# A state-space layer with a mixture of experts: state matrices kept as 64x64 blocks instead of zero-padded 128x128 ones, u in three groups of 128, weights loaded during the scan

## The chip, the core and the metric

The kernel runs on one core of one Trainium2 chip. The time is the device time of one execution in microseconds, and the number given for a kernel is the median of its runs. The engines are TensorE (PE: matmuls; PEld is its weight load), VectorE (DVE), ScalarE (ACT), GpSimd (POOL) and SyncE (SP, which here only issues transfers). All data is fp32, and each fp32 matmul shows as two matmul instructions and two weight loads in the trace.

## The reference

384 tokens of 1024 channels (128 context tokens, 256 latent ones) pass one layer:

```python
mod = silu(cond) @ w_ada + b_ada                   # 1024 x 6144; sh1, sc1, g1, sh2, sc2, g2
h = rms_norm(x, norm_mix) * (1 + sc1) + sh1
u = h @ w_in
x_re, x_im = einsum("blgh,gph->blgp", u_g, bb)     # 64 groups of 16 channels, 64 complex states each
h_t = a * h_(t-1) + x_t                            # forward and backward, complex, diagonal
y = u * d_skip + sum over directions of Re(C h)
m = val * sigmoid(gate),  val, gate = split(gelu(y) @ w_glu)
x = x + g1 * m
x = x + g2 * moe(rms_norm(x) * (1 + sc2) + sh2)    # 16 experts, top 2 of one group, 1024 -> 1024 -> 1024
```

The outputs are the tokens after a final norm and the final states of the context scan. The discretised a and B are computed on the chip from lam, log_dt and b.

## The kernel before

Each engine has its program written out by hand; semaphores join them, and within an engine the order is that of the text. The scan is done over chunks of L = 4 tokens: CC = 32 context chunks and CL = 64 latent ones, C = 96, with one empty column between them CX = 97. 64 groups are held as GP = 32 pairs: the two groups of a pair (index i) lie in partitions 0-63 and 64-127.

Order of the work, by its lines:

1. SyncE loads seven pieces of w_ada (1 MB each), x, the eighth piece, waits for piece seven to land (L287), and loads w_in. ScalarE's own queue loads b, c (each c in two transfers of 256-byte pieces) and ssm_d in eight transfers of single elements (L545 to L557), and only then ScalarE goes on to the squares of the first norm (L564). TensorE multiplies each w_ada piece with silu(cond) (L745), VectorE adds the bias, TensorE spreads the rows to all partitions (L751), VectorE modulates x.
2. TensorE transposes b and x (L782, L794), and makes u = h w_in (L819): for each of the L = 4 positions in a chunk and each half of w_in, 8 matmuls whose weights are the 96 tokens at that position (`hT[:, k, i:T:L]`). Between them it transposes four batches of tables (transpose_W, L809). VectorE meanwhile computes w_pow (w_part) and V (v_part), and last b_keep (L1240). ScalarE copies the transposed W blocks into `pt` (L591), two copies of 64 partitions to a bank.
3. `pt` holds one 128x128 block for each pair, direction and real/imaginary part: the 64x64 blocks of the two groups on its diagonal and zeros elsewhere. GpSimd writes the zeros (zero_blocks, L411 to L421). u is transposed to uT (L837), evicted by ScalarE and VectorE. The P matmuls (L853) then make the chunk inputs, 128x128 weights times 97 columns, and are evicted into S by ScalarE (L624) and VectorE (L1252) in turn.
4. VectorE scans S chunk by chunk (L1265 to L1286). Beside it TensorE makes the kernels K inside a chunk (L870), ScalarE copies them to `kpad` in ring slot 7 (L631), GpSimd adds `dskip`, a diagonal of ssm_d, to them (L432), and SyncE moves them by 32 small transfers into `tmat` (load_T). SyncE loads w_ada pieces 8 to 23 into ring slots 8 to 11, four at a time (L301 to L309), and load_T stands in its queue between pieces 15 and 16.
5. V is copied into zero-padded blocks too, `v_pad`, in ring slots 4 to 11 (L643, eight copies by ScalarE; zeros by GpSimd, L436 and L438); its second half waits for the last w_ada piece.
6. y_inside(k) (L879) multiplies uT by tmat in 64x64 blocks, y_state(k) (L886) adds v_pad times S, read as `S[:, d, d:d + CX, r, g]` with 128 elements from one column to the next. ScalarE applies GELU, TensorE brings the channels into order (L896), the GLU matmuls follow (L954), for which w_glu is loaded into ring slots 4 to 11, each as y_state(k) ends (L320).
7. Norm, routing and 16 experts, whose weights stream through the ring.

## Time and profile before

| | |
|---|---|
| median of 3 runs | 998.11 us (996.9 to 998.47) |
| span of the profiled execution | 997.0 us (the page gives no other time of it) |
| PE busy | 800.8 us, 80% |
| DVE busy | 329.0 us, 33% |
| ACT busy | 195.6 us, 20% |
| POOL busy | 98.2 us, 10% |
| packets under 512 B | 19384 of 78154 |

The span runs from the first to the last instruction. The busy share is an average over all stages: the stages above fill about the first 350 us, the GLU and the routing reach to about 480 us, and the experts take the rest. In the first part each engine has long idle stretches, so the trace is read there in order of time: what starts late, and which event came just before it. In a timeline row the bracket gives the idle time before the work and what ended it.

### The profile page before, as it was taken

What the parts mean: (1) busy time and instruction counts of PE and PEld (TensorE: products, weight loads), DVE (VectorE), ACT (ScalarE), POOL (GpSimd) and SP (SyncE); (2) the same over time, 40 slices, a digit from 0 to 9 for tenths busy, and PEclk for the clock granted to TensorE, in tenths of its full rate; (3) what the DMA queues carried; (4) which work ended last, traced back from release to release, by engine and by line L of the source; (5) the groups of instructions that cost most, each with busy time, mean ns of one, the idle gap of its engine ahead of it and who ended that gap; (6) DMA issues with size and microseconds to landing.
All of it is one profiled execution on the core that took longest, in us unless ns stands there. A gap on an engine that the chain in (4) does not pass through costs nothing.

```text
span 997.0 us, 19297 instructions
## 1 busy us (share of the span) xinstructions
PE 800.8 (80%) x7936; PEld 464.8 (47%) x7937; DVE 329.0 (33%) x894; ACT 195.6 (20%) x372; POOL 98.2 (10%) x109
## 2 busy tenths in 40 slices
PE   4158999970169999965999999999999999999750
PEld 0035668930039944534545455454553555545320
DVE  6149983699910002224021120211111121121116
ACT  0033316300230212210021120211111121121113
POOL 1020002067020010002000000000000000000000
PEclk8579999975579999986999999999999999999995
DMA  8910000440554570047999999999999999999924
GB/s 306 342 14 1 2 0 2 170 171 8 159 214 169 199 273 0 1 165 300 343 397 410 410 410 410 408 410 410 410 410 410 335 413 410 410 411 410 410 74 189
DMA packets 78154, 259.14 MB, mean 260 GB/s; under 512 B 19384, under 2 KB 19816, under 8 KB 73880
## 3 DMA queue, kind: packets, MB, share of 16 engines
q1 hardware_dynamic: 70840, 253.04, 65.0%
q10 hardware_dynamic: 5632, 2.18, 1.3%
q0 software_dynamic: 1632, 3.20, 0.9%
q8 instruction: 38, 0.62, 0.3%
q14 instruction: 12, 0.10, 0.0%
HBM read 252.49 MB, written 6.29 MB: 260 GB/s over the span
## 4 chain that ended last, share of the span: by engine, by line
issue 47%; DVE 3%; POOL 2%; DMA 2%; POOLq 1%; ACT 0%; SPq 0%; DVEq 0%
POOL y_scratch L495 1%; POOLq L513 1%; DMA slots<-slot_list 1%; DMA ring<-y_scratch 0%; DVE ring L1457 0%; DVE sreg L1446 0%; DVE sreg L1447 0%; POOL slot_list L469 0%; DVE sreg L1448 0%; POOL pool_tick L483 0%; DMA slot_list<-sreg,sloti 0%; DMA y_scratch<-vreg,sidx 0%; POOL sidx L488 0%; ACT sreg L723 0%; POOLq L512 0%
## 5 line engine op out<-in xcount | busy, mean ns | idle before, releaser
L995 PE MATMUL ps<-ring,vreg 128*32 128x512 f32 x2240 | 246.6, 599 | 14.1 <-issue 13.8
L995 PEld LDWEIGHTS ps<-ring,vreg 128*32 128x32 f32 x2240 | 74.6, 111 | 179.0 <-issue 179.0
L1017 PE MATMUL ps<-ring,vreg 128*32 128x256 f32 x2240 | 124.2, 380 | 17.0 <-ACT vreg L702 17.0
L1017 PEld LDWEIGHTS ps<-ring,vreg 128*32 128x32 f32 x2240 | 81.3, 110 | 56.0 <-issue 16.3
L745 PE MATMUL ps<-ring,silu_c 128*32 128x512 f32 x192 | 39.6, 925 | 72.8 <-DMA ring<-in_w_ada 72.8
L981 PEld LDWEIGHTS ps<-vreg,sreg 128*128 128x128 f32 x768 | 89.3, 196 | 14.2 <-issue 12.6
L981 PE MATMUL ps<-vreg,sreg 128*128 128x96 f32 x768 | 91.9, 281 | 1.5 <-DVE vreg L1378 1.5
L1408 DVE TENSOR_TENSOR vreg<-vreg,ps 128x256 f32<-128x256 f32 x48 | 17.4, 417 | 224.3 <-ACT vreg L697 224.3
L1418 DVE COPY vreg<-ps 32x256 f32<-32x256 f32 x96 | 40.7, 424 | 132.2 <-PE ps L1017 129.7
L954 PE MATMUL ps<-ring 128*128 128x512 f32 x192 | 83.1, 593 | 0.7 <-ACT ring L652 0.7
L709 ACT ACTIVATE vreg<-ps 32x256 f32<-32x256 f32 x96 | 35.9, 374 | 131.5 <-PE ps L1017 129.5
L819 PE MATMUL ps<-ring,sreg 128*96 128x512 f32 x128 | 58.0, 612 | 1.8 <-ACT sreg L609 1.0
L954 PEld LDWEIGHTS ps<-ring 128*128 128x128 f32 x192 | 36.2, 190 | 45.4 <-issue 44.5
L697 ACT ACTIVATE vreg<-ps 128x256 f32<-128x256 f32 x48 | 15.0, 384 | 210.7 <-PE ps L995 210.7
L745 PEld LDWEIGHTS ps<-ring,silu_c 128*32 128x32 f32 x192 | 4.8, 130 | 104.8 <-DMA ring<-in_w_ada 101.3
L483 POOL TENSOR_TENSOR pool_tick<-ident 1x1 f32<-1x1 f32 x32 | 5.9, 185 | 442.0 <-DVE vreg L1418 357.8
L886 PE MATMUL ps<-sreg,ring 128*128 128x97 f32 x256 | 44.7, 351 | 3.4 <-ACT ring L643 3.4
L1283 DVE TENSOR_TENSOR sreg<-sreg,scan_t 128x128 f32<-128x128 f32 x190 | 46.3, 285 | 1.1
L886 PEld LDWEIGHTS ps<-sreg,ring 128*128 128x128 f32 x256 | 43.8, 219 | 3.8 <-issue 3.6
L1299 DVE TENSOR_TENSOR vreg<-vreg,ps 128x512 f32<-128x512 f32 x6 | 4.1, 689 | 125.1 <-ACT vreg L677 125.1
L819 PEld LDWEIGHTS ps<-ring,sreg 128*96 128x96 f32 x128 | 31.9, 253 | 25.3 <-issue 22.9
L432 POOL TENSOR_TENSOR ring<-ring,dskip 128x256 f32<-128x256 f32 x1 | 36.3, 36312 | 46.3 <-issue 46.3
(257 smaller groups left out, 682.2 us busy)
## 6 DMA issues: line engine op xcount, KB each, us to landing
ring<-in_moe_w_gate SPq DMA_DIRECT2D x128, 512.0 KB, 11.8
ring<-in_moe_w_up SPq DMA_DIRECT2D x128, 512.0 KB, 13.2
ring<-in_moe_w_down SPq DMA_DIRECT2D x128, 512.0 KB
ring<-in_w_ada SPq DMA_DIRECT2D x24, 1024.0 KB, 8.8
ring<-in_ssm_w_glu SPq DMA_DIRECT2D x8, 1024.0 KB, 4.8
ring<-in_ssm_w_in SPq DMA_DIRECT2D x8, 512.0 KB, 12.5
ring<-y_scratch SPq DMA_DIRECT2D x6, 512.0 KB, 6.2
tmat<-ada_rows SPq DMA_DIRECT2D x4, 512.0 KB, 7.1
```

The costliest lines, as they stand in the source:

```text
L432: pool.tensor_tensor(kpad[:, :, :, 48:64], kpad[:, :, :, 48:64], dskip[:, :, :, :], ALU.add).then_inc(pool_k, 1)
L709: act.activation(yrow[32 * t:32 * t + 32, 256 * j:256 * j + 256], src, ACT.Copy).then_inc(y_ev, 1)
L745: last = pe.matmul(ps[ADA_BANK[b]][32 * j:32 * j + 32, :], silu_c[:, k, :], src[:, j * 512:(j + 1) * 512], start=(k == 0), stop=(k == KT - 1))
L819: last = pe.matmul(ps[4 + m % 2][0:C, :], hT[:, k, i:T:L], win[:, k, half * 512:(half + 1) * 512], start=(k == 0), stop=(k == KT - 1))
L886: last = pe.matmul(ps[k][:, q * CX:(q + 1) * CX], v_pad[:, 4 * k + q, d, r, :], S[:, d, d:d + CX, r, 4 * k + q], start=False, stop=(d == 1 ...
L954: last = pe.matmul(ps[2 * (m % 2) + part][:, :], yT[:, k, t * P:(t + 1) * P], ring[:, 4 + k, col:col + 512], start=(k == 0), stop=(k == KT ...
L981: last = pe.matmul(bank[:, col * CAP:(col + 1) * CAP], h2[:, t, k * P:(k + 1) * P], onehot[:, t, :], start=(t == 0), stop=(t == NT - 1))
L995: last = pe.matmul(ps[t][32 * j:32 * j + 32, :], xgT[:, k, 32 * t:32 * t + 32], w[:, :, 256 * j:256 * j + 256], start=(k == 0), stop=(k == ...
L1017: last = pe.matmul(ps[3 + t // 2][32 * dj:32 * dj + 32, 256 * (t % 2):256 * (t % 2) + 256], aT[:, t, c2, 32 * j:32 * j + 32], ring[:, KT + ...
L1283: step(tt(to, to, tb, ALU.add), False)
L1408: tt(act_a[:, t, :], sg[:, t, :], ps[t][:, 256:512], ALU.mult).then_inc(prod_done, 1)
L1418: cp(yrow[32 * t:32 * t + 32, 256 * j:256 * j + 256], src).then_inc(y_ev, 1)
```

## The change

- The state matrices lose their padding. `pt` now holds the 64x64 blocks alone, in ring slots 8 to 11; V is used where it lies. P and y_state take two matmuls of 64 rows and 64 columns for each former one. W's eviction is one copy of 128 partitions, into four banks in turn. The zeroing on GpSimd, the copies L643 and their waits go.
- c is loaded as it lies, one transfer each, and the C transposes become pairs of 64-column matmuls. ssm_d is loaded as 8 rows of 128 early on, and transposed by TensorE (`drow`, `dtab`).
- The skip term: 16 matmuls `i16` by `dskip` add it in PSUM after K; the addition on GpSimd goes.
- The 32 transfers to tmat move from SyncE's queue to ScalarE's, and kpad to ring slot 0.
- w_ada pieces 8 to 23 go to ring slots 4 to 7, and the first of them wait for u only. Half of w_glu is loaded after P, the other half as the last w_ada pieces are used. w_in no longer waits for piece seven.
- u: the tokens of positions 0 to 2 of all chunks form three groups of 96, and the 96 tokens of position 3 are split in three and appended, 32 to each, so that three groups of 128 columns are used. ScalarE's evictions of hT and u become two each.

```diff
-        pads = ring[:, 4:12, :].rearrange("p a b -> p (a b)").rearrange("p (n j) -> p n j", j=P)
-        pt = [pads[:, (1 - d) * 2 * GP:(2 - d) * 2 * GP, :].rearrange("p (g r) j -> p g r j", r=2) for d in range(2)]
-        v_pad = pads.rearrange("p (g d r) j -> p g d r j", d=2, r=2)
+        pt = ring[:, 8:12, :].rearrange("p a b -> p (a b)").rearrange("p (d g r s) -> p d g r s", d=2, g=GP, r=2)
...
-            sp.wait_ge(ld_ada[6], 16)
             for k in range(KT):
                 sp.dma_start(win[:, k, :], w_in[0, k * P:(k + 1) * P, :]).then_inc(ld_win, 16)
...
-            sp.wait_ge(pe_p, 16)
+            def load_glu(k):
+                sp.dma_start(ring[:, 4 + k, :], w_glu[0, k * P:(k + 1) * P, :]).then_inc(ld_glu, 16)
+
+            sp.wait_ge(pe_u, 6)
             for n in range(KT, 3 * KT):
                 b, k = divmod(n, KT)
-                if n == KT + 8:
-                    load_T()
+                if n == KT + 4:
+                    sp.wait_ge(pe_p, 32)
+                    for kk in range(4, KT):
+                        load_glu(kk)
                 if n >= KT + 4:
                     sp.wait_ge(pe_ada, n - 3)
-                sp.dma_start(ring[:, 8 + n % 4, :],
+                sp.dma_start(ring[:, 4 + n % 4, :],
                              w_ada[0, k * P:(k + 1) * P, b * UNIT:(b + 1) * UNIT]).then_inc(ld_late[n % 4], 16)
+            for k in range(4):
+                sp.wait_ge(pe_ada, 2 * KT + k + 5)
+                load_glu(k)
...
-            pool.tensor_tensor(kpad[:, :, :, 48:64], kpad[:, :, :, 48:64], dskip[:, :, :, :], ALU.add
-                               ).then_inc(pool_k, 1)
...
+            act.dma_start(drow[:, 0:P], ssm_d[0].rearrange("(m p) -> m p", p=P)).then_inc(ld_drow, 16)
...
-                for i in range(2):
-                    act.dma_start(cnat[r * DG:(r + 1) * DG, :].rearrange("p (h i s) -> p i h s", h=GS, i=2)[:, i],
-                                  cc.rearrange("a d (g i) h s -> i (a d g) h s", i=2)[i]).then_inc(ld_bc, 16)
-            for q in range(4):
-
-                for i in range(2):
-                    act.dma_start(dtab[32 * q:32 * q + 16, i, :], ssm_d[0].rearrange(
-                        "(m q i h) -> q i h m", m=8, q=4, i=2)[q, i], allow_slow_non_contiguous=True
-                        ).then_inc(ld_dtab, 16)
-
+                act.dma_start(cnat[r * DG:(r + 1) * DG, :], cc.rearrange("a d (g i) h s -> (a d g) (i h s)", i=2)
+                              ).then_inc(ld_bc, 16)
...
-                act.activation(hT[:, k0:k0 + 4, t * P:(t + 1) * P],
-                               ps[m % 2][:, :].rearrange("p (k n) -> p k n", k=4), ACT.Copy).then_inc(act_hT, 1)
+                src = ps[m % 2][:, :].rearrange("p (k c j) -> p k j c", k=4, j=L)
+                to = hT[:, k0:k0 + 4, :].rearrange("p k (a c) -> p k a c", a=3)
+                act.activation(to[:, :, :, 32 * t:32 * t + 32], src[:, :, 0:3, :], ACT.Copy)
+                act.activation(to[:, :, t, 96:P], src[:, :, 3, :], ACT.Copy).then_inc(act_hT, 1)
...
-                    for i in range(2):
-                        a = slice(64 * i, 64 * i + 64)
-                        act.activation(pt[d][a, g0:g0 + 8, r, a],
-                                       ps[2 * (w % 2) + i][a, :].rearrange("p (g s) -> p g s", s=NS), ACT.Copy
-                                       ).then_inc(act_pt, 1)
-            for m in range(8):
+                    act.activation(pt[:, d, g0:g0 + 8, r, :],
+                                   ps[w % 4][:, :].rearrange("p (g s) -> p g s", s=NS), ACT.Copy).then_inc(act_pt, 1)
+            for m in range(6):
...
+            act.wait_ge(act_k, 4)
+            for i in range(2):
+                for j in range(L):
+                    for q in range(4):
+                        dst = tmat[64 * i + 16 * j:64 * i + 16 * j + 16, q:GP:4, :]
+                        act.dma_start(dst, kpad[32 * q:32 * q + 16, i, :, (3 - j) * GS:(7 - j) * GS]
+                                      ).then_inc(ld_tmat, 16)
...
+            for i in range(2):
+                pe.transpose(ps[5][:, 8 * i:8 * i + 8], drow[:, GS * i:GS * i + P], ident[0:8, 0:8])
...
-                    last = pe.matmul(ps[4 + m % 2][0:C, :], hT[:, k, i:T:L], win[:, k, half * 512:(half + 1) * 512],
+                    last = pe.matmul(ps[4 + m % 2][:, :], hT[:, k, i * P:(i + 1) * P], win[:, k, half * 512:(half + 1) * 512],
...
-                        last = pe.matmul(ps[m % 8][:, o:o + CX], pt[d][:, g0 + gi, r, :], uT[:, g0 + gi, :],
-                                         start=True, stop=True)
+                        for i in range(2):
+                            a = slice(64 * i, 64 * i + 64)
+                            last = pe.matmul(ps[m % 8][a, o:o + CX], pt[a, d, g0 + gi, r, :], uT[a, g0 + gi, :],
+                                             start=True, stop=True)
...
+                    for q in range(4):
+                        a = slice(32 * q, 32 * q + 32)
+                        last = pe.matmul(bank[32 * q:32 * q + 16, 0:448].rearrange("p (m w) -> p m w", w=112)[:, :, 48:64],
+                                         i16[a, :], dskip[a, i, 4 * mq:4 * mq + 4, :], start=False, stop=True,
+                                         skip_group_check=True)
...
-                            last = pe.matmul(ps[k][:, q * CX:(q + 1) * CX], v_pad[:, 4 * k + q, d, r, :],
-                                             S[:, d, d:d + CX, r, 4 * k + q], start=False,
-                                             stop=(d == 1 and r == 1), skip_group_check=True)
+                            for i in range(2):
+                                a = slice(64 * i, 64 * i + 64)
+                                v = V[a, d * GP + 4 * k + q, r, 1 - d:5 - d, :].rearrange("p k h -> p (k h)")
+                                last = pe.matmul(ps[k][a, q * CX:(q + 1) * CX], v, S[a, d, d:d + CX, r, 4 * k + q],
+                                                 start=False, stop=(d == 1 and r == 1), skip_group_check=True)
```

## Rows read from the trace of the kernel before

**Rows 1.** The page's 40 slices of 24.9 us: GB/s moved by the transfers.
```profile
GB/s 306 342 14 1 2 0 2 170 171 8 159 214 169 199 273 0 1 165 300 343 397 410 410 410 410 408 410 410 410 410 410 335 413 410 410 411 410 410 74 189
```

**Rows 2.** Timeline, 33 to 64 us: start, duration, engine, line, operation, tiles, count [idle before].
```profile
35.63 1.93 PE L745 MATMUL ps<-ring,silu_c 128*32 128x512 f32 x8 [5.34 <-DMA ring<-in_w_ada]
...
57.55 0.17 DVE L1149 TENSOR_SCALAR stat<-stat 128x3 f32<-128x3 f32 x1 [27.62 <-ACT vreg L564]
...
59.13 9.20 PE L751 MATMUL ps<-ada,ring 128*128 128x512 f32 x16 [21.57 <-DVE ada L1155]
```

**Rows 3.** Timeline of ScalarE, 14 to 60 us: its DMA issues (ACTq).
```profile
17.23 2.96 ACTq L550 DMA_DIRECT2D vreg<-in_ssm_c_re  x2
20.22 14.93 ACTq L547 DMA_DIRECT2D vreg<-in_ssm_b_im  x1
...
44.78 9.11 ACTq L555 DMA_DIRECT2D dtab<-in_ssm_d  x8
```

**Rows 4.** Windows of 5 us: busy us by engine, granted clock, DMA share, GB/s.
```profile
10.00:15.00 5.00, 3.33 (x16) 0.40 (x16) 4.30 (x21) 0.40 (x2) 0.00 (x0) 1.00 1.02 427
...
20.00:25.00 5.00, 2.04 (x16) 0.20 (x8) 4.79 (x41) 0.00 (x0) 0.00 (x0) 0.50 1.06 261
...
35.00:40.00 5.00, 1.93 (x8) 0.20 (x8) 0.00 (x0) 0.00 (x0) 0.00 (x0) 0.50 1.06 374
```

**Rows 5.** Timeline, 112 to 190 us, and the first GLU matmuls.
```profile
112.89 34.66 PE L819 MATMUL ps<-ring,sreg 128*96 128x512 f32 x80
...
144.11 1.23 DVE L1240 COPY tmat<-sreg 128x2048 f32<-128x2048 f32 x1
...
161.13 0.41 DVE L1248 COPY ring<-ps 128x256 f32<-128x256 f32 x1
...
161.65 28.80 PE L853 MATMUL ps<-ring 128*128 128x97 f32 x256 [0.76 <-ACT ring L619]
...
350.90 55.17 PE L954 MATMUL ps<-ring 128*128 128x512 f32 x128 [0.68 <-ACT ring L652]
```

**Rows 6.** Timeline, 190 to 343 us, by engine: VectorE, GpSimd, SyncE, ScalarE, TensorE.
```profile
191.74 0.29 DVE L1275 TENSOR_TENSOR scan_t<-a4r,sreg 128x128 f32<-128x128 f32 x1
...
276.09 0.61 DVE L1283 TENSOR_TENSOR sreg<-sreg,scan_t 128x128 f32<-128x128 f32 x2
...
207.84 36.31 POOL L432 TENSOR_TENSOR ring<-ring,dskip 128x256 f32<-128x256 f32 x1 [46.27 <-issue]
...
244.18 20.70 SPq L297 DMA_DIRECT2D tmat<-ring  x32
...
289.22 7.44 ACT L643 ACTIVATE ring<-vreg 64x2048 f32<-64x2048 f32 x4 [15.11 <-PE ps L745]
...
270.24 1.93 PE L745 MATMUL ps<-ring,silu_c 128*32 128x512 f32 x8 [46.53 <-DMA ring<-in_w_ada]
...
287.62 1.53 PE L745 MATMUL ps<-ring,silu_c 128*32 128x512 f32 x8 [0.53 <-DMA ring<-in_w_ada]
289.08 4.25 PE L879 MATMUL ps<-ring,tmat 64*64 64x97 f32 x96
296.76 33.49 PE L886 MATMUL ps<-sreg,ring 128*128 128x97 f32 x192 [3.43 <-ACT ring L643]
...
337.33 5.58 PE L886 MATMUL ps<-sreg,ring 128*128 128x97 f32 x32
```

**Rows 7.** The x loads (line 284): issues, and microseconds from issue to landing.
```profile
L284 SPq DMA_DIRECT2D vreg<-in_x_sample x2: 445/454/463, 7.9 to 8.4; - x2
...
DMA to landing us min/median/max: 22.4/23.4/24.4
```

**Rows 8.** Windows around the start of y_state: as rows 4.
```profile
293.30:296.70 3.40, 0.03 (x2) 0.00 (x0) 0.00 (x0) 3.38 (x3) 3.08 (x1) 0.81 0.00 0
296.76:299.00 2.24, 2.24 (x11) 2.24 (x11) 0.00 (x0) 1.20 (x1) 0.00 (x0) 0.50 0.00 0
```

**Rows 9.** The page's part 6: issues, KB each, microseconds to landing.
```profile
ring<-in_w_ada SPq DMA_DIRECT2D x24, 1024.0 KB, 8.8
```

100 lines of the change are left out of this document (34 added, 66 removed).

## The prediction, made before the change was timed

> **What bounds the kernel now.** I read the page's slices first. From about 475 us the GB/s row stands near 410 to the end of the experts: that half streams expert weights, and the change touches nothing in it [rows 1]. Before it lies a chain of stages with holes in PE and in the transfers. So I followed the order of time through the first 350 us, engine by engine, and asked at each hole which wait ends last. There are three.
>
> Hole one, 37.6 to 59.1 us. PE has finished the eighth w_ada piece at 35.63 + 1.93 = 37.6, but its next work, the 16 spreading matmuls (L751), starts at 59.13, behind a VectorE chain that waited until 57.55 for ScalarE's squares (L564) [rows 2]. ScalarE was only issuing DMAs: c_re 2.96 us, b_im 14.93, then c_im, and ssm_d 9.11, to 53.9 [rows 3]. These c and ssm_d transfers are cut in pieces of 256 and 4 bytes. While they run the transfers give 261 GB/s at a full share (20 to 25 us) against 427 before [rows 4].
>
> Hole two is not idle: VectorE works from 65 us through the state-space tables to 145.34 (b_keep, L1240), and PE's u matmuls end at 112.89 + 34.66 = 147.55, side by side [rows 5].
>
> Hole three. The scan on VectorE runs from 191.74 to about 276.7; but y_state (L886) starts at 296.76, twenty microseconds later [rows 6]. It waits for ScalarE's copies into the padded blocks (L643, 289.22 + 7.44), which wait for PE's last w_ada piece (287.62 + 1.53), whose loads stood behind the 32 tmat transfers (issued 244.18 to 264.9), which stood behind GpSimd's addition of dskip: one 128x256 operation, 36.31 us long, all of it beside the scan [rows 6].
>
> **The change part by part.**
>
> (a) Contiguous c, ssm_d as one small early transfer. ScalarE's four b and c issues, from about 17 us, should cost some 0.5 to 1.5 us each (two c_re issues took 2.96 us before the queue backed up [rows 3]), so it is free by 19 to 23 us. The squares then wait for x. Without the small packets the transfers should hold 374 to 427 GB/s [rows 4]. The bytes ahead of the end of piece eight are 8.4 MB of w_ada, 1.57 MB of x and about 1 MB of b and c, 11 MB: 26 us at 427, 29 at 374, from about 4 us on: landing at 30 to 33.5 us instead of 35.6. I take 32. Piece eight on PE 1.93, then VectorE's chain to the spread, 59.13 - 57.55 = 1.6 [rows 2]: the spread starts at 35.5, saving 23.6 us; 20 if the piece lands as late as now, 25.5 at the best rate. The squares take 3.6 us (53.9 to 57.55 [rows 2, 3]) and the last of x lands at 8.4 + 24.4 = 32.8, 2.8 us before piece eight [rows 7]; piece eight's 1.93 on PE on top, they fit by 1 us. All 16.4 MB are in by 43 to 48 us; b and c are wanted at 35.5 + 9.2 = 44.7, w_in at 52: even at the late end VectorE, which only needs ScalarE's B copies 2.4 us after they are made now, loses little. The new ssm_d transposes (2 small ones, under 1 us) stand before the first w_ada piece, where PE waits for data anyway.
>
> (b) Three groups of 128, not four of 96. The 80 u matmuls at 34.66 us are 0.433 each [rows 5]; with 128 columns of weights the price is that of the GLU matmuls, 55.17/128 = 0.431. So 32 of 128 instructions go: 13.8 us of PE. From 147.55 that sets the end of u at 133.8 on the old clock of events. Between there and L853 PE has 14.1 us (147.55 to 161.65), of which the last 3 to 4 need uT's evictions: it would come to that point near 144, earlier still since each W eviction is one of 128 partitions, not two of 64. But VectorE ends its tables at 145.34 as now, and then owes half the uT evictions, four pairs of copies whose longer one is 0.41 us [rows 5]: about 2.7 us. So the P matmuls (L853) start at 148.1 instead of 161.65: 13.5 us saved, and VectorE is the bound. The stage could save 13.8 at most and, with 3 us of it lost in the handover between PE and VectorE, some 10.5 at least. The hT evictions become two (384 and 128 elements), about 0.1 us more each, hidden behind VectorE.
>
> (c) P matmuls on 64x64 blocks. 512 instructions instead of 256. The nearest row is y_inside (L879), the same shape from contiguous operands: 96 in 4.25 us, 0.0443 each, so 22.7 us against 28.8. Both ends: 0.0443, or the 0.1125 of today's whole blocks (28.80/256), which would be 57.6 us. I take 0.0443, because it is the same form. PE will have been nearly idle for 3 us ahead of it; after 3.4 us of idleness the clock was granted at 0.50, the 1.2 GHz level, for the next microseconds [rows 8], so I add 2. Saved: 4.1 us. Both eviction engines take turns as now and wait for PE between groups.
>
> A rule speaks against this form. The Trainium skill (TensorEngine Tiling (Array Packing), Restrictions and Gotchas) says that different row tiles cannot access one PSUM bank at the same time. By it (c) and (f) would run one after the other. The y_inside row, whose two row halves write one bank, disagrees: 97 columns at the GLU's 431/512 ns are 82 ns alone, and 44 were measured. What the order of one after the other would cost is R3 below.
>
> (d) Scan: untouched, 85.0 us. Its start moves from 191.74 by 23.6 + 13.5 + 4.1 = 41.2 to 150.5, its end to 235.5.
>
> (e) What must be ready by then. The 512 K matmuls are smaller than y_inside's, so at most 22.7 us, and the 16 skip pieces of 2 instructions about 1 us: they end by 174. Four w_ada pieces are there (their loads need only the u stage), and half of the GLU weights (4 MB, 10 us) load behind them while K runs; the other twelve pieces are fed at (287.62 - 270.24)/7 = 2.48 us a piece [rows 6] after a landing time of some 9 us [rows 9]: 174 + 9 + 11 x 2.48 + 2 = 212. tmat's 32 transfers move to ScalarE's queue, behind which nothing else of ScalarE is due before the scan's end; 20.7 us as now [rows 6], so about 197, or 210 beside the w_ada loads. y_inside 4.3 us: 217. The other half of the GLU weights follows, 10 us more, not needed before the GLU. Slack 18 us at least. GpSimd's zeroing and the L432 addition are gone, and L643 with them. So y_state starts when the scan ends: 235.6 against 296.76. The third hole itself is worth 20.0 of the 61.1 us.
>
> (f) y_state on 64x64 blocks: 512 instructions for 256. Now one costs 33.49/192 = 0.174 us [rows 6], against 0.1125 for L853 with blocks of the same size; what differs is the moving operand (S is read at a stride of 512 bytes). If two row halves run beside each other, as in y_inside, each instruction counts 0.087 and the stage stays at 46.1 us (296.76 to 342.91 [rows 6]). The ends are 0.0443 each, as y_inside, 22.7 us in place of 256 x 0.174 = 44.5 and some 2 lost to the clock at the start: 20 us less; and 0.174 each, 89.1: 44 us more. I take 0.087, no change, since y_inside shows that row halves overlap and L886 that the stride is what costs.
>
> Sum: 23.6 + 13.5 + 4.1 + 20.0 - 0.1 + 0 = 61.1 us off the span of 997.0, so 935.9. The page gives no more than its span; the median of the runs, 998.11, lies 1.1 above it, so 937.0. From 343 us on (pick matmuls, GLU, routing, experts) all shifts as it is.
>
> **The rivals.**
> R1, y_state gets fast: the stride is hidden by two streams in parallel; 937 - 20 = 917. For it: each stream then has only half of the partitions. Against: the stride costs each partition's own read, whatever the height.
> R2, y_state does not overlap at a stride: 937 + 44 = 981. For it: no row shows it overlapping. Against: y_inside.
> R3, the slower side: half-height blocks writing one bank run one after the other, in the P stage (0.1125: 57.6 instead of 24.7, +33) and in y_state (+44). Then 937 + 77 = 1014. It decides as soon as the two stages together cost 61 us more than I put, a mean of 0.125 us an instruction. The y_inside row is against it; only its being an accumulation differs.
> R4, the feed is late: tmat's small packets on ScalarE's queue and w_ada share the engines (c's small packets halved the rate at 20 to 25 us [rows 4]) and both end after the scan. It decides once the feed's 38 us grow by 18; doubled, it overruns by 20: 957.
>
> **How the numbers follow.** Forecast 0.71, its own range 928 to 947 (stage one 20 to 25.5, b and c late up to 3, P stage 1.5 either way, y_state 0.080 to 0.100). R1 0.12, R2 0.09, R3 0.02, R4 0.06. The range takes in R1 and R4 and leaves R2 and R3 out: 915 to 960. Counting a difference only from 0.2%, about what a measurement of this kernel can tell: faster 0.97, the same 0.01, slower 0.02 (R3; 0.01 for a mixture of R2 and R4 that ends near no change).
>
> **What would show it.** L751 at 34 to 39 us; L853 at 123 to 128 with 512 instructions near 0.045 us; VectorE without a gap from the spread to uT; the scan's first step at 149 to 153 and last near 236; no L432; y_state's first matmul within 1 us of the scan's end, 46 us to its last. It would be wrong if y_state waited on tmat or w_ada, or if either half-height stage cost over 0.1 us an instruction.

## The result, and the profile after

The changed kernel takes 966.14 us (median of 4 runs, 964.59 to 968.73), the kernel before 998.29 beside it: ratio 0.9673, 95% interval 0.9646 to 0.9699. The forecast was 937.0, range 915 to 960. So 32 us came where 61 were forecast. The profiled executions show the same: span 965.0 against 997.0, forecast 935.9, 29.1 us short.

Where they went is read in the timeline of TensorE. Columns as in [rows 2].

```profile
42.46 1.93 PE L703 MATMUL ps<-ring,silu_c 128*32 128x512 f32 x8 [8.94 <-DMA ring<-in_w_ada]
46.00 9.87 PE L709 MATMUL ps<-ada,ring 128*128 128x512 f32 x16 [1.61 <-DVE ada L1127]
...
126.17 3.75 PE L775 MATMUL ps<-ident,ring 128*64 128x64 f32 x70 [2.06 <-issue]
...
133.34 2.11 PE L803 MATMUL ps<-ident,ring 96*128 96x96 f32 x12 [1.55 <-DVE ring L1221]
136.21 23.59 PE L819 MATMUL ps<-ring 64*64 64x97 f32 x512 [0.76 <-ACT ring L582]
160.74 4.20 PE L837 MATMUL ps<-vreg,tmat 64*16 64x64 f32 x128 [0.94 <-ACT sreg L587]
...
167.16 5.98 PE L837 MATMUL ps<-vreg,tmat 64*16 64x64 f32 x112 [1.21 <-issue]
173.41 7.13 PE L837 MATMUL ps<-vreg,tmat 64*16 64x64 f32 x128
...
229.84 1.94 PE L703 MATMUL ps<-ring,silu_c 128*32 128x512 f32 x8 [1.10 <-DMA ring<-in_w_ada]
246.37 5.75 PE L851 MATMUL ps<-ring,tmat 64*64 64x97 f32 x96 [14.60 <-DMA tmat<-ring]
251.95 32.09 PE L861 MATMUL ps<-sreg,vreg 64*64 64x97 f32 x384
...
290.55 5.47 PE L861 MATMUL ps<-sreg,vreg 64*64 64x97 f32 x64
...
304.46 15.93 PE L926 MATMUL ps<-ring 128*128 128x512 f32 x33 [0.66 <-ACT ring L610]
```

Set against the forecast, stage by stage (the forecast of an event is its time in [rows 2, 5, 6] less what was to be saved ahead of it):

| event | forecast | measured | late by | of it in this stage |
|---|---|---|---|---|
| spread (L709) | 35.5 | 46.00 | 10.5 | 10.5 |
| P (L819) | 124.6 | 136.21 | 11.7 | 1.2 |
| scan, first step | 150.5 | 161.09 | 10.6 | -1.1 |
| scan, end | 235.5 | 245.63 | 10.1 | -0.5 |
| y_state (L861) | 235.6 | 251.95 | 16.3 | 6.2 |
| y_state, end | 281.8 | 295.95 | 14.1 | -2.2 |
| GLU (L926) | 289.8 | 304.46 | 14.7 | 0.5 |
| end of the span | 935.9 | 965.0 | 29.1 | 14.4 |

Three rows carry it: the first stage, the start of y_state, and the part behind the GLU's start, which was to shift as it is.

The windows of the first stage, to be laid beside [rows 4]: the last two columns are the share of the DMA engines and GB/s. Those engines are full throughout, yet from 21 to 36 us they move 234 to 283 GB/s, little more than half of the 421 before.

```profile
16.00:21.00 5.00, 3.90 (x24) 0.40 (x16) 4.44 (x29) 0.00 (x0) 0.00 (x0) 1.00 1.01 421
21.00:26.00 5.00, 1.69 (x12) 0.16 (x8) 4.83 (x42) 0.00 (x0) 0.00 (x0) 0.82 1.04 283
26.00:31.00 5.00, 0.00 (x0) 0.00 (x0) 3.76 (x24) 0.00 (x0) 0.00 (x0) 0.50 1.01 238
31.00:36.00 5.00, 1.93 (x8) 0.20 (x8) 0.00 (x0) 0.00 (x0) 0.00 (x0) 0.50 1.01 234
36.00:41.00 5.00, 0.00 (x0) 0.00 (x0) 0.00 (x0) 1.09 (x2) 0.00 (x0) 0.50 1.02 382
```

ScalarE's own rows: its issues are short now, and the wait moved to x. Further down, tmat's transfers, which took 20.70 us in [rows 6].

```profile
17.95 0.61 ACTq L520 DMA_DIRECT2D vreg<-in_ssm_c_re  x1
18.59 0.61 ACTq L518 DMA_DIRECT2D vreg<-in_ssm_b_im  x1
...
39.91 1.06 ACT L527 ACTIVATE vreg<-vreg 128x1024 f32<-128x1024 f32 x1 [25.20 <-DMA vreg<-in_x_sample]
...
188.92 53.64 ACTq L602 DMA_DIRECT2D tmat<-ring  x32
```

Behind the GLU's start the expert loop has one hole that the kernel before has not. First the changed kernel, then the one before, at the step from the first expert with three tiles (192 matmuls) to one with two; TensorE's timeline again, and with each the windows around the step.

```profile
570.13 10.57 PE L989 MATMUL ps<-ring,vreg 128*32 128x256 f32 x192 [0.74 <-ACT vreg L660]
588.30 16.88 PE L967 MATMUL ps<-ring,vreg 128*32 128x512 f32 x128 [7.60 <-issue]
```

```profile
580.70:588.30 7.60, 0.00 (x1) 0.01 (x1) 2.54 (x6) 3.52 (x7) 1.13 (x2) 0.72 1.03 402
588.30:593.00 4.70, 4.70 (x24) 1.21 (x28) 0.00 (x0) 0.00 (x0) 0.36 (x2) 0.50 0.25 99
```

```profile
615.41 10.57 PE L1017 MATMUL ps<-ring,vreg 128*32 128x256 f32 x192 [0.74 <-ACT vreg L702]
626.71 13.94 PE L995 MATMUL ps<-ring,vreg 128*32 128x512 f32 x128 [0.73 <-issue]
```

TensorE stands still for 7.6 us and waits for nothing that has a name; behind it the clock is at 0.50 and the transfers pause (99 GB/s), presumably for want of free ring slots. From the first scatter of an expert's rows to the last the loop takes 473.9 us, 460.9 before: 13.0 of the 14.4. The period with the hole is 38.9 us instead of 29.0, the last one 34.1 instead of 30.8, where the matmuls run at a granted clock of 0.82 and 0.81, against 0.91 and 1.00 before. Another 1.5 us are the GLU matmuls, whose first 3.5 us run at 0.56.

### The profile page after: what moved, and what is told of

Its sections match the earlier page's. It is cut to its first block, busy times and chain, and to the rows that moved or that the text cites. A ratio compares the mean times of both kernels' runs of the same rounds, so it can differ in the third digit from the quotient of the medians.

```text
span 965.0 us, 20380 instructions
## 1 busy us (share of the span) xinstructions
PE 802.6 (83%) x8498; PEld 456.4 (47%) x8499; DVE 328.9 (34%) x894; ACT 174.4 (18%) x359; POOL 38.7 (4%) x100
## 4 chain that ended last, share of the span: by engine, by line
issue 50%; DVE 3%; POOL 2%; POOLq 1%; DMA 1%; ACT 0%; SPq 0%; DVEq 0%
POOL y_scratch L464 1%; POOLq L482 1%; POOL slot_list L438 0%; DMA ring<-y_scratch 0%; DVE ring L1430 0%; DVE sreg L1419 0%; DVE sreg L1420 0%; DVE sreg L1421 0%; POOL pool_tick L452 0%; DMA y_scratch<-vreg,sidx 0%; POOL sidx L457 0%; ACT sreg L681 0%; DMA slots<-slot_list 0%; POOLq L481 0%; POOLq L470 0%
## 5 line engine op out<-in xcount | busy, mean ns | idle before, releaser
L967 PE MATMUL ps<-ring,vreg 128*32 128x512 f32 x2240 | 251.2, 608 | 21.0 <-issue 20.7
L926 PE MATMUL ps<-ring 128*128 128x512 f32 x192 | 84.6, 602 | 0.7 <-ACT ring L610 0.7
L703 PE MATMUL ps<-ring,silu_c 128*32 128x512 f32 x192 | 42.0, 976 | 38.6 <-DMA ring<-in_w_ada 38.6
L926 PEld LDWEIGHTS ps<-ring 128*128 128x128 f32 x192 | 36.9, 194 | 46.3 <-issue 45.4
L785 PE MATMUL ps<-ring,sreg 128*128 128x512 f32 x96 | 42.3, 597 | 1.9 <-ACT sreg L572 1.0
L861 PE MATMUL ps<-sreg,vreg 64*64 64x97 f32 x512 | 43.0, 340 | 0.0
L861 PEld LDWEIGHTS ps<-sreg,vreg 64*64 64x64 f32 x512 | 38.8, 149 | 3.4
L1375 DVE COPY vreg<-ps 128x480 f32<-128x480 f32 x16 | 10.5, 657 | 64.7 <-PE ps L953 64.7
L785 PEld LDWEIGHTS ps<-ring,sreg 128*128 128x128 f32 x96 | 17.9, 190 | 23.6 <-issue 21.0
L1248 DVE TENSOR_TENSOR scan_t<-a4r,sreg 128x128 f32<-128x128 f32 x95 | 26.9, 283 | 1.1
## 6 DMA issues: line engine op xcount, KB each, us to landing
ring<-in_moe_w_gate SPq DMA_DIRECT2D x128, 512.0 KB, 10.1
```

The costliest lines, as they stand in the source:

```text
L703: last = pe.matmul(ps[ADA_BANK[b]][32 * j:32 * j + 32, :], silu_c[:, k, :], src[:, j * 512:(j + 1) * 512], start=(k == 0), stop=(k == KT - 1))
L785: last = pe.matmul(ps[4 + m % 2][:, :], hT[:, k, i * P:(i + 1) * P], win[:, k, half * 512:(half + 1) * 512], start=(k == 0), stop=(k == KT ...
L861: last = pe.matmul(ps[k][a, q * CX:(q + 1) * CX], v, S[a, d, d:d + CX, r, 4 * k + q], start=False, stop=(d == 1 and r == 1), skip_group_ch ...
L926: last = pe.matmul(ps[2 * (m % 2) + part][:, :], yT[:, k, t * P:(t + 1) * P], ring[:, 4 + k, col:col + 512], start=(k == 0), stop=(k == KT ...
L967: last = pe.matmul(ps[t][32 * j:32 * j + 32, :], xgT[:, k, 32 * t:32 * t + 32], w[:, :, 256 * j:256 * j + 256], start=(k == 0), stop=(k == ...
L1248: step(tt(tb[0], A4R, chunk_states(f[st], b[st] - f[st], False), ALU.mult), False)
```

## The experiments

Each one is a change to the changed kernel, unless it says "before". Ratios are to the kernel before on the same chip; the changed kernel's is 0.9673.

### The whole again

> The changed kernel once more, unaltered, for a second trace. Its first trace has one hole of 7.6 us in PE between two experts (at 580.7 to 588.3 us) that the kernel before has at none of its expert changes, and the K matmuls at half clock (27 us for 512 where the kernel before needs 15.7). Theory A, both belong to this kernel's code and timing: the hole stands at the same expert again (scatter to scatter 38.9 us at the sixth) and K takes 27 us. Theory B, both are accidents of one execution: no hole or another place, the span 8 us shorter, or K at 16 to 18 us.

965.49 us in one run. Theory A: the hole of 7.7 us, the K stage of 27 us and tmat's 53.4 us all stand where they stood.

### The first stage: which transfers halve the rate

```diff
+            act.wait_ge(ld_x, 16 * NT)
+            for t in range(NT):
+                ...
+                act.activation(scr, x_sb[:, t, :], ACT.Square, ...).then_inc(act_sq, 1)
             act.wait_ge(ld_ada[3], 16)
             for r, (b, cc) in enumerate(((b_re, c_re), (b_im, c_im))):
                 ...
-            act.wait_ge(ld_x, 16 * NT)
-            ...
```

> Changed kernel, but ScalarE issues the four b and c transfers after the squares of the first norm instead of before them. In the changed kernel all transfers together give 218 to 276 GB/s from 21 to 37 us, where 420 were seen before b and c are issued, and the eighth w_ada piece lands at 42.4 instead of the 32 that I predicted. Theory A, the b and c transfers slow the others down: the eighth piece lands at 29 to 32, the spread (L709) starts at 34 to 37 instead of 46.0, and the whole is 5 to 10 us shorter, the rest being given back where PE and VectorE wait for b. Theory B, the rate falls by itself at this point of the queue (reading x, or many transfers outstanding): the eighth piece lands at 40 or later and the whole gets 0 to 5 us longer.

956.05 us, ratio 0.9555 (0.9530 to 0.9579). The rate stays at 396 to 415 GB/s, piece eight is multiplied at 31.27, spread starts at 34.81, 0.7 from the forecast's 35.5. From 36 us on, where b and c now run, it is 234 to 236 GB/s, and TensorE later waits 5.81 us for c_im. The low rate goes with b and c.

```diff
-                act.dma_start(bnat[r * DG:(r + 1) * DG, :], b.rearrange("a d (g i) s h -> (a d g) (i s h)", i=2)
+                act.dma_start(bnat[:, half], b.rearrange("a d (g i) s h -> (a d g i) (s h)", i=2)
...                                                              # c likewise
```

> Changed kernel, but each of the four b and c transfers is written over 128 partitions of 4 KB instead of 64 partitions of 8 KB: same bytes, same issue place. The matrices B and C are thereby scrambled, so the routing and the expert part are not to be compared, only the first 60 us. Theory A1, the slow rate is a matter of 64 destination partitions: the rate at 21 to 37 us returns to about 400 GB/s, the eighth piece lands at 33 to 35, the spread starts at 37 to 39. Theory A2, it is a matter of two queues sharing the engines whatever the partitions: rate and times stay as in the changed kernel (42.4 and 46.0).

944.88 us in one run, a time that can't be compared, since B and C are other numbers and route the tokens otherwise. What counts is the window: the rate is 407 to 416 GB/s from 21 to 41 us. So it hangs on how each transfer is laid over the partitions (here 128 of 4 KB instead of 64 of 8 KB), not on the bytes and not on ScalarE's queue. That left the question whether 64 partitions are too few or the wrong ones:

```diff
-                act.dma_start(bnat[r * DG:(r + 1) * DG, :], b...
+                act.dma_start(bnat[r:P:2, :], b...
...                                                              # c likewise; the evictions put the columns in order
```

> Changed kernel, but b and c are written to every second partition of all 128 (real parts to the even ones, imaginary parts to the odd ones) instead of real to 0-63 and imaginary to 64-127; the evictions of the transposes put the columns back in order. 64 partitions of 8 KB a transfer as now. Writing to 128 partitions took the rate at 21 to 37 us back to 400-430 GB/s and the spread to 40.1. Theory A, what counts is that the 64 partitions span both halves: the same rate, spread at 38 to 41 instead of 46.0, 5 to 7 us off the whole. Theory B, what counts is the number of partitions of a transfer or the size of its pieces: the rate stays at 220 to 280 and the spread at 46.

957.38 us, ratio 0.9596 (0.9560 to 0.9632). It is which ones. The same windows as above, now with b and c in every second partition:

```profile
21.00:26.00 5.00, 2.74 (x12) 0.20 (x8) 4.83 (x42) 0.00 (x0) 0.00 (x0) 1.00 1.01 414
26.00:31.00 5.00, 1.94 (x8) 0.20 (x8) 3.80 (x24) 0.00 (x0) 0.00 (x0) 1.00 1.02 415
31.00:36.00 5.00, 0.00 (x0) 0.00 (x0) 0.00 (x0) 2.32 (x5) 0.00 (x0) 1.00 1.02 416
```

Spread starts at 39.67, 6.3 us earlier. Of the other 4.2 to the forecast, 2.5 are a megabyte of b and c at 415 GB/s: I had counted one ahead of piece eight, and there are two. The last 1.7 are not taken apart.

The Trainium skill (SBUF — State Buffer, Door 1: The DMA port swizzle) says that partitions 0 to 63 and 64 to 127 are reached by different ports, half of them each. By that rule a transfer to partitions 0 to 63, or to 64 to 127, has half the width, and one to every second partition all of it: the traces agree, 234 to 283 GB/s against 414 to 416.

### The skip term alone

```diff
 (before)
-                sp.wait_ge(pool_k, 1)
+                sp.wait_ge(act_k, 4)
...
-            pool.tensor_tensor(kpad[:, :, :, 48:64], kpad[:, :, :, 48:64], dskip[:, :, :, :], ALU.add...
...
+                        last = pe.matmul(bank[32 * q:32 * q + 16, 0:448]..., i16[a, :], dskip[a, i, 4 * mq:4 * mq + 4, :],
```

> Kernel before with one part of the change alone: the skip term added by 16 matmuls after K, the GpSimd addition (36.3 us) gone, the tmat transfers on SyncE's queue waiting for K's evictions. Theory A (my step (e)): the addition was what held tmat, the late w_ada pieces and with them the padded V copies; the tmat issues start at about 209 instead of 244.2, the last w_ada piece ends before the scan, and y_state starts at 277 to 279 instead of 296.8: 18 to 20 us shorter, 978 to 980. Theory B, the padded blocks or their zeroing on GpSimd beside the scan hold y_state as long: GpSimd's 64x4096 memsets or ScalarE's copies end after 290 and less than 10 us are gained.

979.23 us, ratio 0.9791 (0.9773 to 0.9810): by the ratios this one edit brings about 21 of the whole change's 33 us. K takes 17.5 us at the full clock, tmat 21.6 us on SyncE's queue. The third hole of the prediction is gone: y_state waits for the scan alone.

```profile
276.35 33.50 PE L889 MATMUL ps<-sreg,ring 128*128 128x97 f32 x192 [11.96 <-DVEq L1289]
```

There is no hole at the changed kernel's place in its expert loop.

### tmat: the queue, the neighbours, the order

```diff
+            for n in range(KT, KT + 4):
+                ada_piece(n)            # w_ada 8 to 11 ahead of K; one more behind each of its first three banks
```

> Changed kernel, but TensorE multiplies w_ada pieces 8 to 11 right after the P matmuls, before K, and one further piece after each of K's first three banks. In the changed kernel y_state starts at 252.0, 6.2 us after the scan's last step (245.7), since tmat's last transfer lands at 246.3: its 32 issues take 53.6 us of ScalarE's queue (20.7 on SyncE's queue in the kernel before), beside twelve w_ada pieces. Theory A, the two transfer streams slow each other and both are released only by K's end: with the pieces started 20 us earlier, w_ada ends by 212, tmat by 238 at the latest, y_inside is done before the scan's last step, y_state starts 0.1 us after it: 6 us off the whole. Besides, with full-size work ahead of it, K's clock may hold: 16 us instead of 27 for its 512 matmuls. Theory B, tmat's 53 us are the ScalarE queue's own price for such pieces: they take as long without w_ada beside them, and the start of y_state moves only as K's end moves.

962.51 us, ratio 0.9649 (0.9629 to 0.9669). Neither theory in full: tmat was issued later (203.28) and took 37.2 us; y_state started at 248.69. Beside the pieces of w_ada and the w_glu that follows them (to about 233 us) some of its issues take 2.7 to 5.4 us, and from about 232 us on, with the engines to themselves, the median one takes 0.63: ScalarE's queue is not slow by itself. K's first bank ran at the full clock, as in the changed kernel; then TensorE waited 7.34 us for a piece, and the other three ran at half. I needed the transfers wholly by themselves:

```diff
+                    sp.wait_ge(act_k, 4)                   # behind w_glu 4 to 7, ahead of w_ada 12
+                    ...
+                                sp.dma_start(dst, kpad[...]).then_inc(ld_tmat, 16)
...
-            act.wait_ge(act_k, 4)
-            ...
-                        act.dma_start(dst, kpad[...]).then_inc(ld_tmat, 16)
```

> The 32 transfers that fill tmat are issued on SyncE's queue, behind w_glu 4 to 7 and ahead of w_ada pieces 12 to 23, instead of on ScalarE's queue beside them; nothing else is changed. Theory A (tmat's 256-byte packets wait behind w_ada's 8 KB packets in the shared DMA engines): the 32 transfers take about 21 us again, as in the kernel before, instead of 53.6, from about 188 us to 210; the twelve pieces follow at 2.5 to 3.0 us each and end at 240 to 246; y_state starts at the scan's end or up to 6 us later, so 960 us, at most 966. Theory B (the transfers themselves are slower in this kernel, whatever runs beside them): they take 37 to 53 us on SyncE's queue as well, the pieces behind them end at 255 us or later, and the time rises to 975 us or more.

960.10 us, ratio 0.9592 (0.9562 to 0.9622). Theory A for tmat: 20.70 us, the figure of the kernel before to the hundredth. The twelve pieces behind it follow at 2.48 us each, as forecast, not 3.0; the last ends at 245.2, so that y_state starts at 249.24: 2.7 us earlier than in the changed kernel, and 4.3 behind the scan, which ends at 244.90. The ratios differ by more, about 8 us; the rest lies behind y_state and is not taken apart.

```profile
189.49 20.70 SPq L301 DMA_DIRECT2D tmat<-ring  x32
```

### y_state and its stride

```diff
-                                last = pe.matmul(ps[k][a, q * CX:(q + 1) * CX], v, S[a, d, d:d + CX, r, 4 * k + q],
+                                c0 = ((4 * k + q) * 4 + 2 * d + r) * CX
+                                last = pe.matmul(ps[k][a, q * CX:(q + 1) * CX], v, sreg[a, c0:c0 + CX],
```

> Changed kernel, but y_state reads its 97 columns of S from consecutive addresses, not at a stride of 512 bytes (so it multiplies the wrong columns; routing and experts are not to be compared). In the changed kernel one y_state instruction counts 0.084 us, where y_inside counts 0.044. Theory A, the stride alone costs the difference: 0.044 to 0.046 each at full clock, the 384 of the first six in 17 to 19 us instead of 32.1. Theory B, it is the weights in V or the accumulation over eight matmuls: 0.08 and more as now.

943.01 us in one run, again a time that can't be compared, since the routing is another. With neighbouring words (other columns of S, so this leaves the state term undone) an instruction takes 16.30/384 = 0.042 us instead of 0.084, and the stage 23.0 us instead of 44.0. The stride is the whole price, as the prediction's f had it. To have that gain in earnest, S itself must be laid out with its columns innermost:

```diff
-        S = sreg[:, :].rearrange("p (d c r g) -> p d c r g", d=2, c=SLOTS, r=2)
+        S = sreg[:, :].rearrange("p (d r g c) -> p d c r g", d=2, r=2, c=SLOTS)
...                                                              # the scan's addresses accordingly
```

> The state buffer S is laid out with its 98 columns innermost, so that y_state's matmuls and the evictions of P read and write neighbouring words, and the scan's instructions read and write words that stand 98 apart; nothing else is changed. Theory A (a strided fp32 operand costs TensorE twice the time, and VectorE nothing): y_state takes 0.042 us an instruction instead of 0.084, its stage 23 us instead of 44.0, the scan stays at 84.6 us, and the time is about 945 us. Theory B (VectorE pays for the stride too): each of the scan's instructions is longer by a tenth or more, the scan is longer by 8 us or more, up to twice its length, and eats the gain: 953 us to 1030.

977.84 us, ratio 0.9777 (0.9745 to 0.9809): theory B, and slower than the changed kernel. VectorE pays the stride in each of the scan's 380 operations. Half of them, the additions (busy us, mean ns of one), first of the changed kernel, then with columns innermost; the other half went from 283 and 281 to 396 and 394 ns. The last row is y_state, fast but 34 us late.

```profile
L1256 DVE TENSOR_TENSOR sreg<-sreg,scan_t 128x128 f32<-128x128 f32 x190 | 46.2, 282 | 1.1
```

```profile
L1256 DVE TENSOR_TENSOR sreg<-sreg,scan_t 128x128 f32<-128x128 f32 x190 | 66.1, 396 | 1.1
```

```profile
285.79 18.80 PE L861 MATMUL ps<-sreg,vreg 64*64 64x97 f32 x384 [33.24 <-DVEq L1259]
```

> Four things at once, all on the changed kernel: b and c written to every second partition, w_ada pieces 8 to 11 multiplied ahead of K, tmat's transfers on SyncE's queue ahead of pieces 12 to 23 (each half as soon as its two K banks are evicted), and S with its columns innermost. Theory A (the four act apart and add up): spread starts at about 40 us (6 us earlier), tmat and the pieces end before the scan, y_state starts at the scan's end, 239 us, and its stage takes 23 us: 966 less 8, 6 and 21 is about 931 us. Theory B (what one frees another takes back, by the pieces of w_ada ending after the scan): y_state starts 5 us or more after the scan, 936 us or more.

970.56 us, ratio 0.9700 (0.9668 to 0.9733): the layout of S sinks this one too. tmat and the pieces are done by 228.7, but the scan ends only at 279.

### Four groups instead of three

```diff
-            for m in range(6):
+            for m in range(8):
...
-                    last = pe.matmul(ps[4 + m % 2][:, :], hT[:, k, i * P:(i + 1) * P], win...
+                    last = pe.matmul(ps[4 + m % 2][0:C, :], hT[:, k, i:T:L], win...
```

> The changed kernel with u again in four groups of 96 columns instead of three of 128; nothing else is changed. Theory A (the forecast's step b: the third of the groups that went is worth what P gained): P starts at about 149 us instead of 136.2 and the time is about 978 us. Theory B (VectorE's work on the loads of b and c, not u, sets the start of P): P starts at 138 us or before, and the time is within 2 us of 966.

968.11 us, ratio 0.9699 (0.9678 to 0.9719). P starts at 143.73, 7.5 us later, and the intervals of the two ratios overlap: no difference is clear of the noise, and neither theory holds. Two things make up for it. P itself is 2 us shorter (21.64 against 23.59), as the clock does not dip at its start. And K keeps the full clock (4.2 us for 128 matmuls, not 7.13), so tmat is issued at 185.77 instead of 188.92 and lands with the scan's end: y_state starts at 251.32 against 251.95. In the changed kernel what the three groups bring is lost at tmat.

```profile
143.73 21.64 PE L815 MATMUL ps<-ring 64*64 64x97 f32 x512 [0.76 <-ACT ring L578]
...
180.69 4.21 PE L833 MATMUL ps<-vreg,tmat 64*16 64x64 f32 x128
...
251.32 32.12 PE L857 MATMUL ps<-sreg,vreg 64*64 64x97 f32 x384 [0.31 <-DVEq L1255]
```

### The clock in K

K ran at the full clock in the kernel before, in e4_skip_alone, e7_groups96 and e16_best_96, and at half for most of it in the sixteen others. With three groups TensorE is ahead of VectorE and stands idle before P, with four it does not; so I suspected the idle stretch. Each kernel has one trace, only the changed one's code two. The windows (granted clock third from the right) of the changed kernel, then of e7_groups96:

```profile
125.00:130.00 5.00, 3.83 (x71) 3.71 (x72) 4.97 (x2) 1.24 (x3) 0.00 (x0) 0.66 1.01 423
130.00:136.00 6.00, 3.91 (x32) 3.43 (x32) 4.78 (x16) 2.73 (x9) 0.33 (x2) 0.78 0.04 12
...
170.00:175.00 5.00, 5.00 (x94) 4.61 (x91) 5.00 (x26) 0.55 (x1) 0.00 (x0) 0.50 0.31 125
```

```profile
130.00:136.00 6.00, 6.00 (x126) 4.59 (x127) 2.98 (x7) 2.22 (x4) 0.00 (x0) 1.00 0.38 124
...
170.00:175.00 5.00, 4.40 (x134) 4.02 (x130) 5.00 (x26) 0.54 (x1) 0.00 (x0) 1.00 1.02 424
```

But two kernels that were run for other questions speak against it. In e2_bc_late TensorE waits only 0.87 and 0.76 us ahead of P, the clock stays at 1.00 and P takes 21.64 us, and yet K falls to half:

```profile
125.00:130.00 5.00, 3.37 (x62) 3.03 (x62) 3.15 (x11) 2.07 (x6) 0.47 (x2) 1.00 0.10 33
...
160.00:165.00 5.00, 5.00 (x94) 4.61 (x91) 5.00 (x26) 0.54 (x1) 0.00 (x0) 0.50 0.28 110
```

e14_before_nops (below) has no such stretch either, and TensorE's work ahead of K is the same as in the kernel before, row for row. First the kernel before, then e14_before_nops:

```profile
180.00:190.00 10.00, 10.00 (x92) 10.00 (x92) 4.72 (x6) 4.61 (x6) 0.00 (x0) 1.00 0.78 328
190.00:200.00 10.00, 9.01 (x288) 8.88 (x288) 9.35 (x45) 1.47 (x3) 0.00 (x0) 1.00 0.01 3
```

```profile
180.00:190.00 10.00, 10.00 (x92) 10.00 (x91) 4.82 (x6) 4.51 (x6) 0.00 (x0) 1.00 0.79 333
190.00:200.00 10.00, 9.01 (x195) 8.87 (x196) 9.25 (x45) 1.06 (x2) 0.00 (x0) 0.67 0.01 3
```

K takes 25.3 us there, 15.7 before. So the idle stretch is not needed for the fall, and what decides it is not in these rows. K's 64x16 blocks run at either level; which one stays open.

```diff
-            sp.wait_ge(pe_u, 6)
+            sp.wait_ge(pe_uT, 8)
```

> The changed kernel, whose SyncE waits with w_ada pieces 8 to 11 until u is transposed (the wait on pe_u becomes one on pe_uT), so that no transfer runs beside the transposes of W and u from 116 to 130 us. Theory A (TensorE's holes without a releaser stand beside transfers that fill the DMA engines, since its instructions come by them, and the clock falls because of the holes): the hole of 2.06 us at 124 us is gone, the granted clock does not fall ahead of P, and K keeps the full clock for longer than 4.2 us; if it keeps it to the end, tmat starts 11 us earlier and the time is about 960 us. Theory B (holes and clock have nothing to do with the transfers): a hole of 2 us ahead of P, K 27 us, 966 us.

966.10 us, ratio 0.9657 (0.9630 to 0.9683). Theory A for the hole, B for the clock: with no transfers beside it the 2.06 us hole at 124 us is gone (119.58, 7.68 us, without a break), but TensorE just waits for VectorE instead (5.44 us), the clock dips all the same, and K takes 27 us. So that hole needs transfers beside it. They do not make it alone: e7_groups96 has 423 GB/s beside the same transposes (135 to 140 us) and no hole. The dip ahead of P does not need them. Beside K they ran here too (419 GB/s from 165 to 170 us); but in e14_before_nops the clock fell between 193 and 194 us with 3 GB/s from 190 to 200, so K's fall does not need them either.

### The hole in the expert loop

```diff
+            for n in range(128):        # e9_nops: ahead of the wait for tmat; e13_nops300: 300, at the head
+                pe.nop()
```

> Changed kernel with 128 empty instructions on TensorE, in the idle time before the wait for tmat. Three traces of the changed kernel's code have a hole of 7.5 to 7.7 us in PE, each where the two-tile path of an expert is entered again after the first three-tile expert; the kernel before has 0.7 us there. Theory A, the hole depends on where the expert code lies in TensorE's instruction stream (562 more matmul instructions stand ahead of it in the changed kernel): with the 128 ahead the hole moves, shrinks or goes; if it goes the whole is 7 to 9 us shorter. Theory B, it does not depend on the place: the same hole at the same expert change and the same time within 0.3%.

968.60 us, ratio 0.9689 (0.9657 to 0.9722), hole 7.63.

> 300 instructions that do nothing are put ahead of TensorE's first one, where it waits for data; nothing else is changed. Theory A (the hole of 7.6 us in the expert loop hangs on where the code of the loop lies, by more than the 128 instructions tried before move it): the hole is gone or stands at another expert, and the time falls to about 958 us. Theory B (it does not hang on the position): the hole of 7.6 us stays at the first two-tile expert behind a three-tile one, 966 us.

963.64 us in one run, hole 7.88. Both theory B: shifting the loop's code by 128 or 300 instructions does nothing.

> The kernel before, with 562 instructions that do nothing ahead of TensorE's first one, so that its program is as long as the changed kernel's. Theory A (the length of the program ahead of the loop makes the hole of 7.6 us): a hole of 7 us or more stands ahead of the first two-tile expert behind a three-tile one, and the time is about 1006 us. Theory B (the hole does not hang on the length): no hole above 1 us there, 998 us.

999.12 us in one run, and 0.65 us at the place of the hole: theory B, the length of the program isn't it. Its K at half clock, above, ends 9.7 us later and yet costs nothing, and that sets a reading of the prediction right. GpSimd's addition of dskip, which waits for K, starts at 217.55 instead of 207.84 and ends at the same moment, 244.25 against 244.15 in [rows 6]:

```profile
217.55 26.70 POOL L432 TENSOR_TENSOR ring<-ring,dskip 128x256 f32<-128x256 f32 x1 [55.88 <-issue]
```

In both traces this is where VectorE's stream of scan operations first breaks, after 32 steps of eight operations (at 243.60 and 243.70 us), and passes to four a step. So the 36.31 us are not the operation's own price: it looks as if it could end only once VectorE paused. Two traces show that; no run was made for it.

```diff
+                with pe.If(n <= 64):
+                    expert(e, last_of_round, 2)
                 with pe.If(n > 64):
                     expert(e, last_of_round, TT)
```

> The changed kernel with the two branches of TensorE's expert loop in the other order, the one for two tiles first; nothing else is changed. Theory A (the hole is the first jump from the three-tile branch back to the loop's head and its fetch): it stays ahead of the expert behind the first three-tile one, 7 to 8 us, and the time is 966 us. Theory B (the hole is the first passing over one branch to the other): it goes or moves to another expert, and the time is 958 to 966 us.

964.86 us in one run. Theory B in part: with the branches in the other order the hole behind the three-tile expert is gone, but two others stand earlier, 7.20 and 7.70 us, ahead of the second and third expert. The time stays, since one more is gone: ahead of the last expert the changed kernel has a hole of 5.78 us, and here there is none. That one the kernel before has too, so holes of this kind are not the changed kernel's alone. First e15_two_first, ahead of the third expert, then the kernel before, ahead of the last:

```profile
500.81 15.79 PE L967 MATMUL ps<-ring,vreg 128*32 128x512 f32 x128 [7.70 <-issue]
```

```profile
937.89 15.23 PE L995 MATMUL ps<-ring,vreg 128*32 128x512 f32 x128 [5.80 <-issue]
```

Of three windows of 5 us from 575 on in the changed kernel, the one in which the hole begins (580 to 585) has two of these packets, beside a queue of weights at 99.1%, and the others one each:

```profile
q1 hardware_dynamic: 539, 1.96, 99.1%
q8 instruction: 2, 0.03, 3.7%
```

The Trainium skill (Advanced Engine Details and Errata, ISA Cache) gives the instruction cache lines of 16 KB, 256 instructions each; the packet size agrees. That the hole is a wait for such a packet is not shown: the kernel before has one too in the window ahead of the same step (620 to 625 us), beside weights at 101.5%, and a hole of 0.73 us.

```profile
q8 instruction: 1, 0.02, 1.4%
```

Why the changed kernel stands still there and the kernel before does not stays open: there was a hole of 6.5 to 7.9 us in every kernel derived from the changed one, and none of that size in the kernel before and the two derived from it.

### The best version

Even partitions for b and c, w_ada 8 to 11 multiplied ahead of K, and tmat on SyncE's queue in two halves:

```diff
+                    for i in range(2):
+                        sp.wait_ge(act_k, 2 * i + 2)
+                        ...
+                                sp.dma_start(dst, kpad[32 * q:32 * q + 16, i, :, (3 - j) * GS:(7 - j) * GS]
```

> Three things at once on the changed kernel: b and c written to every second partition, w_ada pieces 8 to 11 multiplied ahead of K, and tmat's transfers on SyncE's queue ahead of pieces 12 to 23, each half as soon as its two K banks are evicted. S keeps its layout. Theory A (the late feed cost 6.2 us at the scan's end and the slow loads 6.3 us at the start, and both add up): spread at about 40 us, P at about 129.7, the scan ends at about 239, y_inside is done by 234, y_state starts at the scan's end, 13 us earlier than in the changed kernel: 953 us. Theory B (an earlier feed is given back in the expert loop or before it): 957 us or more.

948.28 us (5 runs, 947.09 to 952.79), ratio 0.9496 (0.9478 to 0.9515), 18 us better than the changed kernel. y_inside is done before the scan, and y_state's releaser is VectorE at the scan's end:

```profile
229.67 6.01 PE L853 MATMUL ps<-ring,tmat 64*64 64x97 f32 x96
239.65 32.13 PE L863 MATMUL ps<-sreg,vreg 64*64 64x97 f32 x384 [3.97 <-DVEq L1261]
```

It is even 5 us below the 953 expected; its profiled execution (952.79) is the slowest of the five and fits the sum. The hole is still there (7.92). Then four groups put back into it:

> The kernel of e12b_best (even partitions for b and c, w_ada 8 to 11 ahead of K, tmat on SyncE's queue) with u in four groups of 96 columns again. Theory A (three groups bring P forward by 7.5 us, and in the changed kernel tmat alone ate that, since with four groups the clock holds through K and tmat is 3.6 us earlier): with tmat out of the way the 7.5 us show, P starts at about 137.5 instead of 129.9, and the time is about 955 us against 948.3. Theory B (three groups bring nothing anywhere): 946 to 950 us.

957.60 us, ratio 0.9589 (0.9555 to 0.9623): theory A. With tmat out of the way P 7.0 us later (136.94), itself 2.1 us shorter at a clock that does not dip, costs 4.9 at y_state, which starts at 244.53. The ratios differ by 0.0093, 9.3 us, the two profiled spans, 955.0 and 951.0, by 4.0; the intervals don't meet. So three groups are worth something here, 4.9 us at y_state by the traces, and nothing that is clear of the noise in the changed kernel.

## Why the prediction was wrong

The sign and the parts were right; the sum failed in two of its steps and in the sentence that closes it. Two causes are shown by experiments; the third, the largest, is only located.

**(a) failed in its size: 13.1 us, not 23.6.** "Without the small packets the transfers should hold 374 to 427 GB/s" was the mis-sized term. It laid the 261 GB/s in [rows 4] to the packets of 256 and 4 bytes. Without them the windows give 283, 238 and 234, on the mean no more, so nothing shows that the small packets were a reason. What is shown is that b and c go to 64 neighbouring partitions, and that stayed. With that removed in e10_bc_even the spread comes 6.3 us earlier; with b and c out of the way in e2_bc_late it comes at 34.81. Another 2.5 us are the second megabyte of b and c, which the sum left out.

**(b) held: 1.2 us too much.** The stage from spread to P took 90.2 us against 89.0. VectorE was the bound, as said. The three groups are 6.9 of the stage's 12.3 us (97.1 with four in e7_groups96, 102.5 in the kernel before); the other 5.4 came with the rest of the change, and were not taken apart.

**(c) held.** 23.59/512 = 0.046 us an instruction against 0.0443, and P to scan 1.1 us less than forecast. The rule of the Trainium skill (TensorEngine Tiling (Array Packing), Restrictions and Gotchas) that row tiles can't use one PSUM bank at a time is not borne out: R3 put 0.1125 on one after the other, and it falls.

**(d) held**, 84.5 us against 85.0.

**(e) failed: this is R4, at a third of its price.** Counted from the scan's first step, K ended at +27.1 instead of +23.5, as its clock fell (27 us, not at most 23.7); and tmat's transfers took 53.64 us, not 20.7. By themselves they take 20.70 (e8_tmat_sp, on SyncE's queue; on ScalarE's own a lone issue takes 0.62 us, e5_ada_first), so the other 33 us come from the 8 KB packets of w_ada, and of the w_glu behind it, in the same engines, as R4 described it. I had them end at 197, or 210 "beside the w_ada loads", 21 us ahead of where they could hurt; R4 then needed the whole feed to double, while tmat's part alone grew 2.6 times. y_state started 6.2 us after the scan, where R4 had put 20.

**(f) held**: 0.084 us an instruction, 44.0 us the stage, against 0.087 and 46.1. e6_s_contig shows that it is the stride: R1's stage of 23 us is real, but only for contiguous columns. The 0.084 itself, half of the 0.174 of the kernel before, shows that row halves overlap at a stride too, so R2 falls.

**"From 343 us on all shifts as it is" failed by 14.4 us.** 9.8 are the expert with the hole (6.9 of them the hole, 7.60 against 0.73, and 2.9 its matmuls at a lower clock, 16.88 against 13.94), 3.3 the last expert and about 1.5 the GLU, both at a lower clock. The hole comes back in every trace of this code; of the last expert's 3.3 us the second trace has 1.2 in the matmuls, so part of it is that execution's. e14_before_nops and e15_two_first show that neither the program's length nor one particular jump makes the hole; what does stays open. It was a term of the sum with no bound on it, and the range had no room for it: with the shortfall ahead of the GLU alone, 14.7 us, the time would have been 951.7, inside the range.

## What to carry to other kernels

Before moving transfers to a second queue, ask what shares the DMA engines with them: small packets beside large ones took 2.6 times as long, and on the large ones' own queue, ahead of them, no longer than by themselves. Check which partitions a load reaches, not only how long its packets are. And a stage that is made faster only pays once the next thing in line is out of the way: undo the part both in the changed kernel and in one where that next thing is mended.
